# A two-block transformer kernel: residuals in PSUM at both memory borders, rotary halves by transfers

## What is computed

```
x = x + 0.5 * rms_norm(swiglu(rms_norm(x)))        # first block, feed-forward 1
x = x + rms_norm(hybrid_mixer(rms_norm(x)))        # differential + sparse attention, 'proj1' .. 'out1'
x = x + 0.5 * rms_norm(swiglu(rms_norm(x)))        # feed-forward 2
for i in 0, 1:                                     # second block
    mem_k, mem_v = rmsnorm(mem) @ w_mem_kv[i]      # 256 memory tokens
    y_main = gated short convolution (i = 0) or stick-breaking attention (i = 1)
    x = x + concat(y_main, memory_attention(q_mem, mem_k, mem_v)) @ w_o[i]
    x = x + swiglu(rmsnorm(x))                     # (after i = 0 also k, v of the stick-breaking attention)
return rmsnorm(x)
```

## Time and profile before

| | us |
|---|---|
| median of 3 runs | 2310.27 (2309.74 to 2311.41) |
| the profiled execution | 2309.9 |
| its span, first to last instruction | 2307.8 |
| TensorE busy | 2234.9 (97%) |
| VectorE, ScalarE, GpSimd busy | 944.0, 823.8, 974.6 |
| mean granted clock of TensorE | 0.986 |

### The profile page before, as it was taken

The page is one execution under the profiler, slowest core; times in us unless marked ns, Lnnn a source line. Parts: engine busy times, 40 slices in busy tenths (PEclk is TensorE's granted clock), DMA queues, the critical chain, the costliest instruction groups (busy, mean ns, idle before and its releaser), DMA issues.

```text
span 2307.8 us, 28179 instructions
## 1 busy us (share of the span) xinstructions
PE 2234.9 (97%) x10366; PEld 1771.7 (77%) x10366; DVE 944.0 (41%) x1289; ACT 823.8 (36%) x1362; POOL 974.6 (42%) x435
## 2 busy tenths in 40 slices
PE   8999999999998999999999999999999889999997
PEld 6888887875556788888777888888877568888886
DVE  3211346356874411234675311134552653111345
ACT  4222335324873322223532422223342654222222
POOL 4444444553003544444443454444443434544442
PEclk9999999999998999999999999999999899999999
DMA  5222232432001322323232232222222002322221
GB/s 188 91 95 105 91 111 89 127 110 74 1 1 55 110 91 91 104 97 109 73 110 73 82 118 91 101 100 91 91 91 75 17 1 92 109 100 100 91 93 70
DMA packets 29799, 202.66 MB, mean 88 GB/s; under 512 B 3360, under 2 KB 4000, under 8 KB 6048
## 3 DMA queue, kind: packets, MB, share of 16 engines
q1 hardware_dynamic: 28800, 198.55, 24.5%
q10 hardware_dynamic: 928, 3.14, 0.4%
HBM read 198.54 MB, written 2.10 MB: 87 GB/s over the span
## 4 chain that ended last, share of the span: by engine, by line
PE 69%; DVE 4%; ACT 1%; issue 1%; POOL 1%; DVEq 0%; ACTq 0%; POOLq 0%
PE PS L946 20%; PE PS L948 20%; PE PS L947 20%; PE PS L1377 1%; PE PS L1238 1%; PE PS L1197 1%; PE PS L1269 1%; DVE NMAX L1667 1%; PE PS L1361 1%; PE PS L1389 1%; DVE ACC L1434 1%; PE PS L1017 0%; POOL X L479 0%; PE PS L1220 0%; DVE TMP L1514 0%
## 5 line engine op out<-in xcount | busy, mean ns | idle before, releaser
L454 POOL TENSOR_TENSOR WL<-RAW,WH 128x1024 fp32r<-128x1024 f32 x368 | 908.5, 2473 | 1234.4 <-ACT WH L521 1234.4
L946 PE MATMUL PS<-XH,WH 128*128 128x512 f32 (+1 forms) x2200 | 865.9, 394 | 28.9 <-DVE XL L1426 19.8
L948 PE MATMUL PS<-XH,WL 128*128 128x512 f32 (+1 forms) x2200 | 853.2, 388 | 0.0
L947 PE MATMUL PS<-XL,WH 128*128 128x512 f32 (+1 forms) x2200 | 852.8, 388 | 0.0
L521 ACT ACTIVATE WH<-RAW 128x1024 fp32r<-128x1024 f32 x368 | 388.1, 1059 | 1255.4 <-PE PS L948 1211.2
L946 PEld LDWEIGHTS PS<-XH,WH 128*128 128x128 f32 x2200 | 415.4, 189 | 125.1 <-issue 27.6
L947 PEld LDWEIGHTS PS<-XL,WH 128*128 128x128 f32 x2200 | 415.7, 189 | 86.6 <-issue 4.1
L948 PEld LDWEIGHTS PS<-XH,WL 128*128 128x128 f32 x2200 | 415.3, 189 | 84.8
L946 PE MATMUL PS<-HH,WH 128*128 128x512 f32 x672 | 261.4, 389 | 0.0
L947 PE MATMUL PS<-HL,WH 128*128 128x512 f32 x672 | 261.4, 389 | 0.0
L948 PE MATMUL PS<-HH,WL 128*128 128x512 f32 x672 | 261.4, 389 | 0.0
(11 more groups left out here) (194 smaller groups left out, 1558.2 us busy)
## 6 DMA issues: line engine op xcount, KB each, us to landing
RAW<-wstream SPq DMA_DIRECT2D x183, 1024.0 KB, 4.8
X<-xT SPq DMA_DIRECT2D x4, 512.0 KB, 9.0
WORK<-memT ACTq DMA_DIRECT2D x2, 1024.0 KB, 5.4
outT<-WORK SPq DMA_DIRECT2D x8, 256.0 KB, 2.1
RAW<-wstream SPq DMA_DIRECT2D x2, 512.0 KB, 6.3
PB<-WORK ACTq DMA_DIRECT2D x8, 127.8 KB, 2.3
CST<-consts SPq DMA_DIRECT2D x1, 912.0 KB, 10.6
WORK<-constsb SPq DMA_DIRECT2D x1, 256.0 KB, 12.4
```

The lines of the kernel that those rows point to most:

```text
L454: pool.tensor_tensor(WL[:, s, :, :].rearrange("p a b -> p (a b)"), RAW[:, s, :], WH[:, s, :, :].rearrange("p a b -> p (a b)").bitcast(F), ...
L946: pe.matmul(o, wh, xh, start=start, stop=False)
L947: pe.matmul(o, wh, xl, start=False, stop=False)
L948: return pe.matmul(o, wl, xh, start=False, stop=stop)
```

## The change

Six edits go together.

1. *Borders.* A new `post_mem` on VectorE writes the scaled chunk and then X plus that chunk into PSUM (bank `XBANK[k]`), all eight chunks on VectorE; GpSimd's `update_x` stays for out1 alone. ScalarE (`pre_norm_mem`) takes XH from PSUM and later copies each new chunk back to X; units 0 and 1 of the next projection and the transposes of mem wait for these copies.
2. *Order and banks there.* `down0` and `down1` finish their banks in the order 5, 6, 7, 0 to 4. ScalarE copies 5, 6, 7; the memory units share banks 5 and 6, half a bank each; sums of squares use banks 6 and 7; VectorE takes the memory units in pairs. VectorE makes no copy of bank 0.
3. *Rotary halves.* `PERM` goes. After VectorE has scaled a rotary unit, ScalarE issues four transfers of 8 partitions each, which put the halves crosswise into `LT`; the sign is in the SIN table, and the other partitions of LT are zero from a memset at the start.
4. *Early steps.* The scores of the stick-breaking steps 0 to 3 and what follows them up to the low parts are placed ahead of, or beside, the last kv unit. kv units 8 to 11 use banks 2, 3, 6, 7, and sv4 and sv5 are transposed into their own banks.
5. *GpSimd's order.* Low parts 0 to 7 come before the weight splits of units 2 and 3 of outB.
6. The table of constants is 256 columns narrower.

```diff
-X_ON_DVE = {"down0": (0, 2, 4, 6), "out1": (0,), "down1": (0, 2, 4, 6)}
+X_ON_DVE = {"down0": tuple(range(KC)), "out1": (0,), "down1": tuple(range(KC))}
+Y_ORDER = {"down0": (5, 6, 7, 0, 1, 2, 3, 4), "down1": (5, 6, 7, 0, 1, 2, 3, 4)}
+XBANK = (0, 1, 2, 3, 4, 7, 5, 6)
+SB_AHEAD = 4
...
+            split_units(0, U0["gu1"] + POOL_X_AT)
+            update_x("out1")
+            split_units(U0["gu1"] + POOL_X_AT, U0["outB"] + 2)
+            low_softplus(0, 8)
+            split_units(U0["outB"] + 2, U0["outB"] + RING)
+            low_softplus(8, len(SBSTEPS))
...
+            def pre_norm_mem(name, part, mem):
+                n = KC * POSTS_MEM.index(mem)
+                def copy_back(k):
+                    act.wait_ge(xn_ready, KC * XN["proj1" if mem == "mem0" else "projA"] + k + 1)
+                    act.activation(X[:, k, :], PS[:, XBANK[k], :], ACT.Copy).then_inc(xc_done, 1)
+                for k in range(KC):
+                    if k == 0:
+                        refill(mem, 1, 0)
+                    if k == 2:
+                        refill(mem, 1, 1)
+                    if k == 4:
+                        unit(U0[mem] + 3)
+                    x_wait(act, part, k)
+                    act.activation(XH[:, k, :], PS[:, XBANK[k], :], ACT.Copy, scale=gain(name, k)
+                                   ).then_inc(xh_ready, 1)
+                    if k:
+                        copy_back(k - 1)
+                copy_back(KC - 1)
+                refill(mem, 2, 2)
+                squares(name, lambda k: X[:, k, :], KC, lambda k: act.wait_ge(xc_done, n + k + 1))
...
+            def rotate(x):
+                act.wait_ge(taken, x["t"] + 1)
+                for a in (0, DH):
+                    for b in (0, 8):
+                        act.dma_start(LT[a + b:a + b + 8, x["c"] % 2, :],
+                                      SQ[a + 8 - b:a + 16 - b, x["f"] % 2, :]).then_inc(rotated[x["c"] % 2], 16)
...
+                    if part == "kv" and n == len(jobs) - 1:
+                        turn(jobs[n - 2])
+                        for t in range(SB_AHEAD):
+                            sb_exp_ln(t)
...
+                    if x["kind"] in ROTARY:
+                        rotate(x)
...
+                    if k == 0 and copied is not None:
+                        pe.wait_ge(xc_done, copied + bank + 1)
...
-                if x["kind"] in ROTARY:
-                    mm = pe.matmul(PS[:, 4 + f % 2, :], PERM, SQ[:, f % 2, :], start=True, stop=True)
...
+                        if part == "kv" and i == len(jobs) - 1:
+                            pe.wait_ge(taken, jobs[i - 2]["t"] + 1)
+                            for t in range(0, SB_AHEAD, 2):
+                                sb_pair(t)
...
+            for t in range(SB_AHEAD, n + LAG_V, 2):
+                if SB_AHEAD < t < n:
+                    sb_pair(t)
                 if 0 <= t - LAG_T < n:
                     sb_tail(t - LAG_T)
                     sb_tail(t + 1 - LAG_T)
+                if t == SB_AHEAD:
+                    sb_pair(t)
+                    flip(JOBS["kv"][-1])
...
+            def post_mem(name, part, stage, nxt, mem):
+                add_squares(name)
+                dve.wait_ge(rstd_ready, NIDX[name] + 1)
+                n = KC * POSTS.index(part)
+                for k in range(KC + 1):
+                    if k < KC:
+                        y, bank = PS[:, k, :], PS[:, XBANK[k], :]
+                        if k in YC:
+                            dve.wait_ge(y_copied, 3 * POSTS_MEM.index(mem) + k - 4)
+                            y = YC[k]
+                        dve.scalar_tensor_tensor(bank, y, gain(name, k), RSTD[:, :],
+                                                 ALU.mult, ALU.mult).then_inc(y_scaled, 1)
+                        dve.wait_ge(y_scaled, n + k + 1)
+                        dve.tensor_tensor(bank, X[:, k, :], bank, ALU.add).then_inc(xd_ready, 1)
+                    if k >= 1:
+                        low(stage, nxt, k - 1, PS[:, XBANK[k - 1], :])
+                    if k in (2, 4):
+                        for j in (k - 2, k - 1):
+                            take_mem(JOBS[mem][j], j, JOBS[mem][k - 1])
+                add_squares(nxt)
...
-                dve.wait_ge(flipped, f + 1)
-                chain(dve.tensor_tensor(TMP[:, 1, :], SIN, PS[:, 4 + f % 2, :], ALU.mult))
+                dve.wait_ge(rotated[x["c"] % 2], 64 * ((x["c"] + 1) // 2))
+                chain(dve.tensor_tensor(TMP[:, 1, :], SIN, LT[:, x["c"] % 2, :], ALU.mult))
...
+                if t < KC - 1:
+                    dve.wait_ge(xh_used, (KC - 1) * XH_USERS.index("kv") + t + 1)
```

More of the change, by code:

```diff
@@ L106, in bank_of @@
         return dict(slot=slot, bank=n % 4, free=t - 3 if n >= 4 else 0, after=False)
+    if part == "kv" and slot >= 16:
+        return dict(slot=slot, bank=slot - (14 if slot < 18 else 12), free=0, after=True)
     if slot >= 18:
@@ L142 @@
 FLIPS = {x["f"]: x for v in JOBS.values() for x in v if "f" in x}
+for _f, _x in FLIPS.items():
+    _x["clear"] = max([FLIPS[g]["c"] for g in range(_f % 2, _f, 2) if FLIPS[g]["kind"] in TURNED], default=0)
 XN = {n: i for i, n in enumerate(
@@ L354, in program @@
         flipped = sem("flipped")
+        rotated = [sem(f"rotated{i}") for i in range(2)]
         turned = sem("turned")
@@ L591, in post_norm @@
             def post_norm(name, part):
                 def ready(k):
-                    if part.startswith("out"):
-                        refill(part, 1, k)
+                    refill(part, 1, k)
                     if k == 0:
[L597 to L603, removed]
@@ L605, in post_norm, with post_norm_mem, after @@
-                squares(name, lambda k: PS[:, k, :] if k else Y0[:, :], KC, ready, after=after)
+                        act.wait_ge(y0_done, 1)
+                squares(name, lambda k: PS[:, k, :] if k else Y0[:, :], KC, ready)
+                rstd(name, KC, 0)
+            def post_norm_mem(name, part):
+                order = Y_ORDER[part]
+                def after(n):
+                    if order[n] in YC:
+                        act.activation(YC[order[n]], PS[:, order[n], :], ACT.Copy).then_inc(y_copied, 1)
+                squares(name, lambda n: PS[:, order[n], :], KC, lambda n: y_wait(act, part, order[n]), after)
@@ L606, in post_norm @@
                 if part == "down0":
                     rstd_mem()
[L608 to L612, removed]
+                refill(part, 1, FC - 2)
+                rstd(name, KC, 7)
+                refill(part, 1, FC - 1)
             def round_o(chunks, ready):
@@ L620, in x_updated, with x_normed @@
                 return lambda k: act.wait_ge(x_ready, KC * XU[stage] + k + 1)
[L622 to L631, removed]
+            def x_normed(part):
+                return lambda k: x_wait(act, part, k)
             def xh_left(part, stage):
@@ L811, in project @@
                     round_unit(x["u"] + RING)
-                    if n >= 2 and jobs[n - 2]["kind"] in TURNED:
+                    if n >= 2 and jobs[n - 2]["kind"] in TURNED and not (part == "kv" and n == len(jobs) - 1):
                         turn(jobs[n - 2])
@@ L893, in _ @@
             tables()
-            post_norm("ff2_post", "down1")
-            pre_norm("mixA", x_normed("down1", "mem1"), middle=lambda: refill("mem1", 2, 2),
-                     late=lambda: [turn(y) for y in JOBS["mem1"][2:]])
+            post_norm_mem("ff2_post", "down1")
+            pre_norm_mem("mixA", "down1", "mem1")
             project("projA")
@@ L909, in _ @@
             n = len(SBSTEPS)
[L910 to L916, removed]
             def sb_weights(t):
@@ L1064, in down @@
                     have(u0 + k)
+                order = Y_ORDER.get(f"down{l}", range(KC))
                 for c in range(KC + LAG_C):
-                    for k, bank in ((FC - 2, c), (FC - 1, c - LAG_C)):
-                        if not 0 <= bank < KC:
+                    for k, n in ((FC - 2, c), (FC - 1, c - LAG_C)):
+                        if not 0 <= n < KC:
                             continue
+                        bank = order[n]
                         if k == FC - 1:
-                            if bank == 0:
+                            if n == 0:
                                 pe.wait_ge(last_ready, l + 1)
@@ L1163, in project @@
                         mem_step(MEM_BESIDE[part], k)
-                if "f" in jobs[-1]:
+                if jobs[-1]["kind"] in TURNED and part != "kv":
                     flip(jobs[-1])
@@ L1170, in scores @@
                     pe.wait_ge(roped, 10)
+                    pe.wait_ge(taken, TAKEN["proj1"] - 1)
+                if part == "mix1" and y["s"] == 2:
+                    pe.wait_ge(taken, TAKEN["proj1"])
                 if y["p"] == 4 * 4:
@@ L1617, in project @@
                         next_input(part, False)
+                    if last and part == "kv":
+                        for t in range(SB_AHEAD):
```

(2 more changed lines are left out.)

302 lines of the change are left out of this document (145 added, 157 removed).

## The result

The forecast was 2291 us, 0.8% faster. The kernel with the change takes **2316.67 us** (median of 10 runs) against 2310.35 of the kernel before (10 runs beside it): ratio 1.0026, 95% interval 1.0016 to 1.0036. It is a little slower, and outside the range. One run of each kernel was far slower (3174.9 and 6142.1 us); the ratio leaves it out. The profiled execution took 2316.7, its span 2314.8, 7.0 longer than before.

A forecast was written before the change was run, and what follows sets the result against it. TensorE, busy 97% of the span, was taken as the bound; 10.7 - 1.0 - 1.1 + 4.3 + 4.9 + 1.5 = 19.3 us off 2309.9, plus 0.4 to the median, gives 2291 us, range 2282 to 2303 (8 in 10).

The forecast's parts named there:

- Borders, 4.3 + 4.9: At the two memory borders the sum-of-squares matmul comes earlier: 4.3 us gained at the first, 4.9 at the second.
- Flips, 10.7: Fourteen PERM matmuls leave TensorE; twelve before the end of the last unit, 0.89 us each, gain 10.7 us.
- raw_hidden now stands behind the issues of nq1: On ScalarE the hidden copy queues behind transfer issues while turning matmuls after nq2 want it: 1.0 us lost, 0 to 5.
- up to 10.5: Rotation loop of take, issue, landing, product and sum: 6.84 us against a 6.86 period, up to 10.5 with collisions.
- the free banks: Three free banks, some 16 us, were to absorb the lag of the rotation loop.
- Issue and landing: Each rotation transfer was taken at 0.62 us to issue and 2.3 us to landing, 6.2 at worst.
- Start of attention, 1.1 lost: After the last projection unit the rotation chain is exposed before the first maximum: 1.1 us lost, 0 to 5.
- Early steps, 1.5: First stick-breaking scores move ahead of the last kv unit: net 1.5 us gained, -1 to 4.4.
- the transfers set the pace: Rival, 7%: with landings of 6.2 us and colliding sums the rotations run about 24 us late at the first maximum, 2315 us.
- The main case: All terms together give 2291 us, own range 2286 to 2298, chance 66%.
- The prediction's own test: Wrong if TensorE waits over 5 us in the projections for `taken` or the hidden copy; border signs were named too.

The follow-up runs named there:

- e5: Changed kernel with the PERM matmuls back, no early steps and GpSimd's old order at the output projection: 2297.73 us, ratio 0.9957 to the kernel before.
- e9: e3 with the rotation transfers issued from SyncE's queue: 2286.98 us, ratio 0.9911 to the kernel before.
- e1: Changed kernel with the PERM matmuls back in place of the transfers, all else as changed: 2297.61 us, ratio 0.9962 to the kernel before.
- e8: Changed kernel with the four transfers of each rotation issued from SyncE's queue between weight loads: 2296.70 us, ratio 0.9951 to the kernel before.
- e3: Changed kernel with PSUM operands, so no VectorE rotation instruction has two SBUF inputs: 2294.13 us, ratio 0.9946 to the kernel before.
- e2: Changed kernel with the raw_hidden copy moved ahead of the rotation of ks and nq1 on ScalarE: 2311.71 us, ratio 1.0011 to the kernel before.
- e6: e3 with raw_hidden ahead of the rotation of ks and nq1, as in e2: 2295.83 us, ratio 0.9946 to the kernel before.

## Why the prediction was wrong

Point by point, by its own steps:

- **Borders, 4.3 + 4.9**: right. 4.35 and 4.75 us between the sum-of-squares matmuls of either side, 9.1 of the 11.2 us of e5.
- **Flips, 10.7**: right on TensorE (10.4 in proj1, e9 against e1). The ledger of proj1 above has it in the kernel after too, under the new waits.
- **"raw_hidden now stands behind the issues of nq1 ... I take 1.0 us lost (0 to 5)"**: this is the step that failed. 21.9 us of waits, and some 4.7 of low clock after them. It counted what stands in front of `raw_hidden` as 2.5 us of issues. In front of those issues is a wait for VectorE, and the price of a place behind it is VectorE's lag. The lag was in the text, as a loop of "up to 10.5" against 6.86; the trace has 10.1 to 10.5 (takes at 457.9, 468.4, 478.7, 488.8), which is 3.4 behind per rotation, 11.8 by ks. It was set against the free banks, and they did absorb it: no unit waited for a bank. What the step left out is the second road, ScalarE's own order, and that it has two victims, since `raw_hidden` also stands behind ks. e8 (other queue) and e3 (no collisions) each remove most of it, by 20.0 and 22.5 us; e2 and e6 show that moving `raw_hidden` alone does not. What stays open is how e8's 20 us divide between the free line and the collisions that went with it.
- **Issue and landing**: the sizes were right: 0.63 us per issue for 0.62; to landing after the last issue 1.4 us in six of the nine places where VectorE waited for it, 2.0 in two and 4.4 in one, for 2.3. In e3 it was up to 4.2.
- **Start of attention, 1.1 lost**: the first maximum stands 7.1 us after the last unit, 6.4 before: 0.7.
- **Early steps, 1.5**: the marks shift by 2.8, the runs with and without the steps differ by 0.1 and 1.5; not resolved, and small. The stretch gains 3.5 us in e5, which has no early step, so its gain lies for the most part elsewhere: in the kv banks, whose change the prediction held at nothing, and in the clock; no run separates these two.
- **The rival "the transfers set the pace" (7%, 2315 us)** had the right sign and time, 2316.7, by a different mechanism: it wanted landings of 6.2 us, "decides from a landing of about 5 us on", and the loss at the first maximum. Landing was 1.4 to 4.4, collisions of both instructions did what it gave to landing, and the loss came in mid-stage. Its condition did not occur and its time did, by luck: the half of it that was true, the sum colliding, got no chance of its own.

The main case and this rival differ in what a lag meets. The prediction's own test, "wrong if TensorE waits for ... the hidden copy within the projections for more than 5 us", named the place exactly; the price was not worked out.

## What to carry to other kernels

When a transfer that waits for engine A is put on the queue of engine B, everything behind it on B inherits A's lag: list what B owes the bottleneck in the next 10 us, or issue from an engine that owes nothing (here SyncE, 20 us of difference for the same transfers, fewer collisions included). A lag that banks can absorb is absorbed on one road only; follow each road by which the lagging engine reaches TensorE. And a VectorE instruction added beside GpSimd work wants one input in PSUM.

## What the runs showed of the hardware

- An engine that waits ahead of its own DMA issue does nothing else: ScalarE went 8.1 to 8.6 us without a copy five times, issues included, while `raw_hidden` and refills stood next in its program. The Trainium skill (Trainium Kernel Development and Optimization, "Key Constraints") says that issuing from several engines only saves the sequencer's issue time; moving the issue (2.6 us per rotation) to SyncE saved 20 us here. How much of that is issue time and how much the wait ahead of it, no run separates; in the 8.06 us before `raw_hidden` at 492.15 it is 2.6 and 5.4.
- Four transfers of 8 partitions x 512 fp32 took 2.62 us to issue and 1.4 to 4.4 us more to land in the kernel after.
- VectorE's sum with one input in PSUM took 0.69 us 14 times of 14 in e3, 13 of them beside a split of GpSimd; the sine product with both in SBUF up to 2.9.
- The granted clock was 0.50 in the stretch behind 11.7 us without matmuls, and 0.64, as the mean of 4.4 us, behind 10.2.
